# First attention of a two-block kernel: carried sums on VectorE, fewer triangle and mask matmuls

## The reference

```python
def stick_breaking_core(q, k, v):
    for start in range(0, seq, QBLK):            # QBLK = 128
        end = start + QBLK
        z = einsum('bhtd,bhsd->bhts', qf[:, :, start:end], kf[:, :, :end]) * scale
        earlier = arange(end)[None, :] < arange(start, end)[:, None]
        log_keep = where(earlier, log_sigmoid(-z), 0.0)
        csum = cumsum(log_keep, axis=-1)
        log_w = log_sigmoid(z) + (csum[..., -1:] - csum)
        w = where(earlier, exp(log_w), 0.0)
        outs.append(einsum('bhts,bhsd->bhtd', w, vf[:, :, :end]))
```

## Time and profile before

| | us |
|---|---|
| median of 3 runs | 1557.08 |
| lowest and highest | 1555.89, 1557.33 |
| span of the profiled execution | 1554.5 |
| PE busy in it | 1453.5 (94%) |
| ACT, POOL, DVE busy | 639.7, 760.4, 568.8 |

### The profile page before, as it was taken

One profiled execution on the slowest core, in us unless ns is written; L12 is line 12 of the kernel. 1 busy time (PEld: TensorE's weight loads), 2 busy tenths in 40 slices (PEclk: granted clock), 3 DMA queues, 4 the chain that ended last, 5 costly groups with the idle time before them and its releaser, 6 DMA issues.

```text
span 1554.5 us, 23458 instructions
## 1 busy us (share of the span) xinstructions
PE 1453.5 (94%) x8892; PEld 1181.3 (76%) x8892; DVE 568.8 (37%) x649; ACT 639.7 (41%) x1030; POOL 760.4 (49%) x591
## 2 busy tenths in 40 slices
PE   6999999898998999999999799599989999999995
PEld 6878778676776888888887477488867887888874
DVE  2024233244244333333122549732339334121222
ACT  4455465335335444444222645234334332222332
POOL 5734324245235655565555345753309554444563
PEclk9999999999999999999999899799999999999998
DMA  6412111022111332323333122100002332333322
GB/s 233 144 58 68 53 51 58 27 96 66 56 54 59 108 102 96 94 94 95 108 108 95 54 82 82 41 3 3 3 28 82 96 122 81 95 96 97 101 87 81
DMA packets 33772, 122.80 MB, mean 79 GB/s; under 512 B 3745, under 2 KB 4001, under 8 KB 33441
## 3 DMA queue, kind: packets, MB, share of 16 engines
q1 hardware_dynamic: 32832, 119.03, 23.7%
q10 hardware_dynamic: 864, 2.68, 0.5%
HBM read 119.59 MB, written 2.10 MB: 78 GB/s over the span
## 4 chain that ended last, share of the span: by engine, by line
PE 83%; DVE 9%; issue 4%; ACT 2%; POOL 2%; DMA 1%; DVEq 0%; ACTq 0%; POOLq 0%; SPq 0%
PE ps L421 19%; PE ps L423 19%; PE ps L422 19%; PE ps L529 3%; PE ps L943 2%; PE ps L447 2%; PE ps L448 1%; PE ps L1021 1%; PE ps L1022 1%; PE ps L1023 1%; PE ps L931 1%; PE ps L437 1%; PE ps L769 1%; PE ps L511 1%; PE ps L501 1%
## 5 line engine op out<-in xcount | busy, mean ns | idle before, releaser
L1501 POOL TENSOR_TENSOR w_lo<-stage,w_hi 128x512 fp32r<-128x512 f32 x434 | 604.1, 1415 | 664.7 <-ACT w_hi L1055 664.7
L1055 ACT ACTIVATE w_hi<-stage 128x512 fp32r<-128x512 f32 x434 | 249.8, 623 | 456.7 <-DMA stage<-w 452.2
L421 PE MATMUL ps<-x_hi,w_lo 128*128 128x512 f32 x1080 | 425.7, 394 | 6.0 <-POOL w_lo L1501 3.3
L423 PE MATMUL ps<-x_hi,w_hi 128*128 128x512 f32 x1080 | 421.2, 390 | 0.0
L422 PE MATMUL ps<-x_lo,w_hi 128*128 128x512 f32 x1080 | 420.9, 390 | 0.0
L421 PEld LDWEIGHTS ps<-x_hi,w_lo 128*128 128x128 f32 x1080 | 203.2, 188 | 52.7 <-issue 6.3
L422 PEld LDWEIGHTS ps<-x_lo,w_hi 128*128 128x128 f32 x1080 | 203.2, 188 | 43.3 <-issue 1.7
L423 PEld LDWEIGHTS ps<-x_hi,w_hi 128*128 128x128 f32 x1080 | 203.1, 188 | 42.7
L1807 DVE SCALAR_TENSOR_TENSOR conv<-ps,vcol,conv 128x511 f32<-128x511 f32 x44 | 33.0, 749 | 146.9 <-ACT conv L1205 146.9
L2043 DVE TENSOR_TENSOR bt<-gates,ps 128x512 f32<-128x512 f32 x24 | 16.4, 681 | 146.4 <-PE ps L1023 146.4
L421 PE MATMUL ps<-f_hi,w_lo 128*128 128x512 f32 x176 | 68.9, 391 | 0.0
(11 more groups left out here) (316 smaller groups left out, 2363.7 us busy)
## 6 DMA issues: line engine op xcount, KB each, us to landing
stage<-w SPq DMA_DIRECT2D x217, 512.0 KB, 3.5
H<-xT SPq DMA_DIRECT2D x1, 2048.0 KB, 13.7
outT<-H SPq DMA_DIRECT2D x8, 256.0 KB, 2.0
mem<-memT SPq DMA_DIRECT2D x2, 512.0 KB, 6.7
pool_n<-pool_count ACTq DMA_DIRECT2D x1, 1024.0 KB, 4.9
w_small<-small ACTq DMA_DIRECT2D x1, 512.0 KB, 5.0
con<-const ACTq DMA_DIRECT2D x1, 448.0 KB, 4.9
scan_keep<-const ACTq DMA_DIRECT2D x1, 256.0 KB, 9.2
```

Of the source, the lines that this page charges most:

```text
L421: pe.matmul(out, wl, hi(k), start=first, stop=False)
L423: mm = pe.matmul(out, wh, hi(k), start=False, stop=end)
L1055: act.activation(w_hi[:, b % RING, cols], stage[:, b % RING, cols], ACT.Copy).then_inc(whi_made, 1)
L1501: pool.tensor_tensor(w_lo[:, b % RING, cols], stage[:, b % RING, cols], w_hi[:, b % RING, cols].bitcast(F32), ALU.subtract).then_inc(wlo_m ...
```

## The change

The four regions stand in another order: region 3 (128 columns) now lies between region 0 and region 1 in the same bank as before. The parts of the change are:

- Masks: `never` is now two masks side by side, so that the first columns of regions 3 and 1, which are neighbours, are masked by one matmul of 256 columns: three matmuls a head in place of four. ACT makes the second copy of the mask once (a fifth step of `mask_made`).
- Sums within a block: the triangle `suffix` is applied to all 1280 columns in matmuls of 512, 512 and 256 columns, for the high and the low part (six). Region 3 into region 2 is added by two of 128 columns.
- Sums of later blocks: DVE adds keep of region 3 into the matching columns of region 2, and that into region 1, in place; then it splits these 640 columns into `later_hi` and `later_lo` (four new DVE instructions a head, each behind a semaphore of its own), and PE applies `every` to them, two matmuls of 256 and two of 384 columns, behind the new wait on `sb_llo`. A head has 12 matmuls in place of 20.
- `keep` has one buffer for both heads, since the buffer of head 1 is used by `later_hi` and `later_lo`. Head 1 may start only when `sb_llo` of head 0 is there, and the value copy stands behind `sb_llo` of head 1.
- The two DMAs of `levels` and `scan_keep` (used in the second block) move from the start of ACT's stream to behind the last pair.

The diff, without the lines that only declare semaphores:

```diff
@@ -69,8 +69,10 @@
 POOL_WINDOWS = (2, 4, 8, 16)
 
 
-REGION = {0: (0, 512), 1: (512, 384), 3: (896, 128), 2: (1024, 256)}
+REGION = {0: (0, 512), 3: (512, 128), 1: (640, 384), 2: (1024, 256)}
 SCORES = 1280
+DIAGONALS = [(0, P), (REGION[3][0], 2 * P), (REGION[2][0], P)]
+LATER0, LATER = REGION[1][0], 5 * P
 
 
 def build_block(nc, w, xT, memT, vec, const, small, pool_count, outT):
...
@@ -96,8 +98,8 @@
         vcol = at("vcol", [P, VEC], 99.5)
         suffix = at("suffix", [P, P], 24, F32R)
         every = at("every", [P, P], 24.5, F32R)
-        never = at("never", [P, P], 25, F32R)
-        ident_r = at("ident_r", [P, P], 25.5, F32R)
+        never = at("never", [P, 2, P], 25, F32R)
+        ident_r = at("ident_r", [P, P], 31, F32R)
         tmp = at("tmp", [P, 2, SEQ], 101.5)
         acc = at("acc", [P, SEQ], 105.5)
         acc2 = at("acc2", [P, SEQ], 107.5)
...
@@ -118,7 +120,9 @@
         vT_sb = at("vT_sb", [P, SEQ], A0 + 52)
         v_sb = at("v_sb", [P, NS, P], A0 + 54)
         soft = [at(f"soft{h}", [P, SCORES], 80 + 5 * h) for h in range(2)]
-        keep = [at("keep0", [P, SCORES], 90), at("keep1", [P, SCORES], A0 + 56)]
+        keep = at("keep", [P, SCORES], 90)
+        later_hi = [at("later_hi0", [P, LATER], 26, F32R), at("later_hi1", [P, LATER], A0 + 56, F32R)]
+        later_lo = [at("later_lo0", [P, LATER], 28.5, F32R), at("later_lo1", [P, LATER], A0 + 58.5, F32R)]
         keep_hi = [at(f"keep_hi{h}", [P, SCORES], A0 + 61 + 5 * h, F32R) for h in range(2)]
         keep_lo = [at(f"keep_lo{h}", [P, SCORES], A0 + 71 + 5 * h, F32R) for h in range(2)]
         xq = at("xq", [P, KB, SEQ], A0 + 48)
...
@@ -487,7 +495,7 @@
 
 
             E = EV0["sb"] + CREDIT
-            pe.wait_ge(mask_made, 4)
+            pe.wait_ge(mask_made, 5)
             pe.wait_ge(mv_taken, 8 + CREDIT)
             pe.wait_ge(h_split, 1)
 
...
@@ -512,23 +520,28 @@
                                   q_sb[64 * h:64 * h + 64, SEQ - n:SEQ], start=(i != 3), stop=False,
                                   skip_group_check=True)
                 for h in range(2):
-                    for i in range(NS):
-                        o, n = REGION[i]
-                        mm = pe.matmul(scores(h)[:, o:o + P], ident_r[:], never[:], start=False, stop=False,
-                                       skip_group_check=True)
+                    for o, n in DIAGONALS:
+                        mm = pe.matmul(scores(h)[:, o:o + n], ident_r[:], never[:].rearrange("p a n -> p (a n)")[:, 0:n],
+                                       start=False, stop=False, skip_group_check=True)
                     mm.then_inc(sb_scored, 1)
 
             def later_sums(g, h):
                 pe.wait_ge(sb_klo, 2 * g + (h + 1))
-                for i in range(NS):
+                for o, n in ((0, 512), (512, 512), (1024, 256)):
+                    for part in (keep_hi, keep_lo):
+                        pe.matmul(scores(h)[:, o:o + n], suffix[:], part[h][:, o:o + n], start=False, stop=False,
+                                  skip_group_check=True)
+                o, n = REGION[2]
+                for part in (keep_hi, keep_lo):
+                    pe.matmul(scores(h)[:, o + P:o + n], every[:], part[h][:, REGION[3][0]:REGION[3][0] + P],
+                              start=False, stop=(part is keep_lo), skip_group_check=True)
+                pe.wait_ge(sb_llo, 2 * g + (h + 1))
+                for i in (1, 0):
                     o, n = REGION[i]
-                    for s in range(i, NS):
-                        so, sn = REGION[s]
-                        m = suffix if s == i else every
-                        for part in (keep_hi, keep_lo):
-                            mm = pe.matmul(scores(h)[:, o + n - sn:o + n], m[:], part[h][:, so:so + sn],
-                                           start=False, stop=(s == NS - 1 and part is keep_lo),
-                                           skip_group_check=True)
+                    ro, rn = REGION[i + 1]
+                    for part in (later_hi, later_lo):
+                        mm = pe.matmul(scores(h)[:, o + P:o + n], every[:], part[h][:, ro - LATER0:ro - LATER0 + rn],
+                                       start=False, stop=(part is later_lo), skip_group_check=True)
                 mm.then_inc(sb_summed, 1)
 
             def turn_v(g):
...
@@ -1041,8 +1054,6 @@
         def _(act):
             act.dma_start(con[:], const[:, 0:C0["levels"]]).then_inc(params_in, 16)
             act.dma_start(vcol[:], vec).then_inc(params_in, 16)
-            act.dma_start(levels[:], const[:, C0["levels"]:C0["scan"]].rearrange("p (l n) -> p l n", n=HB)).then_inc(levels_in_s, 16)
-            act.dma_start(scan_keep[:], const[:, C0["scan"]:CONST]).then_inc(levels_in_s, 16)
             act.preload_act_table_set("natural_log_exp_and_others")
             act.sem_inc(evac, CREDIT)
 
...
@@ -1076,7 +1087,8 @@
             act.activation(suffix[:], C("suffix"), ACT.Copy).then_inc(mask_made, 1)
             act.activation(every[:], C("all"), ACT.Copy).then_inc(mask_made, 1)
             act.activation(ident_r[:], ident, ACT.Copy).then_inc(mask_made, 1)
-            act.activation(never[:], C("never"), ACT.Copy).then_inc(mask_made, 1)
+            act.activation(never[:, 0, :], C("never"), ACT.Copy).then_inc(mask_made, 1)
+            act.activation(never[:, 1, :], C("never"), ACT.Copy).then_inc(mask_made, 1)
 
             def pair(g, i, b, first=False, last=False):
 
...
@@ -1119,6 +1131,9 @@
                 pair(2 * i + 2, i, U0["sb"] + 8)
             pair(PAIRS - 1, 0, U0["sb"] + 3 * PAIRS - 1, last=True)
 
+            act.dma_start(levels[:], const[:, C0["levels"]:C0["scan"]].rearrange("p (l n) -> p l n", n=HB)).then_inc(levels_in_s, 16)
+            act.dma_start(scan_keep[:], const[:, C0["scan"]:CONST]).then_inc(levels_in_s, 16)
+
             def square_of(n, k, p):
 
                 act.wait_ge(y_made, k + (1 + CREDIT + BEFORE["y_made"][n]))
...
@@ -1689,13 +1704,25 @@
                 for h in range(2):
 
                     dve.wait_ge(sb_ln, 2 * g + (h + 1))
-                    dve.scalar_tensor_tensor(out=keep[h][:], in0=scores(h)[:, 0:SCORES], scalar=0.0, in1=soft[h][:],
+                    dve.scalar_tensor_tensor(out=keep[:], in0=scores(h)[:, 0:SCORES], scalar=0.0, in1=soft[h][:],
                                              op0=ALU.max, op1=ALU.add).then_inc(sb_keep, 1)
                     dve.wait_ge(sb_keep, 2 * g + (h + 1))
-                    dve.tensor_copy(keep_hi[h][:], keep[h][:]).then_inc(sb_khi, 1)
+                    dve.tensor_copy(keep_hi[h][:], keep[:]).then_inc(sb_khi, 1)
                     dve.wait_ge(sb_khi, 2 * g + (h + 1))
-                    dve.tensor_tensor(keep_lo[h][:], keep[h][:], keep_hi[h][:].bitcast(F32),
-                                      ALU.subtract).then_inc(sb_klo, 1)
+                    dve.tensor_tensor(keep_lo[h][:], keep[:], keep_hi[h][:].bitcast(F32), ALU.subtract).then_inc(sb_klo, 1)
+                    dve.wait_ge(sb_klo, 2 * g + (h + 1))
+                    o3, o2, o1 = REGION[3][0], REGION[2][0], REGION[1][0]
+                    dve.tensor_tensor(keep[:, o2 + P:o2 + 2 * P], keep[:, o2 + P:o2 + 2 * P], keep[:, o3:o3 + P],
+                                      ALU.add).then_inc(sb_from2, 1)
+                    dve.wait_ge(sb_from2, 2 * g + (h + 1))
+                    dve.tensor_tensor(keep[:, o1 + P:o1 + 3 * P], keep[:, o1 + P:o1 + 3 * P], keep[:, o2:o2 + 2 * P],
+                                      ALU.add).then_inc(sb_from1, 1)
+                    dve.wait_ge(sb_from1, 2 * g + (h + 1))
+                    dve.tensor_copy(later_hi[h][:], keep[:, LATER0:SCORES]).then_inc(sb_lhi, 1)
+                    dve.wait_ge(sb_lhi, 2 * g + (h + 1))
+                    dve.tensor_tensor(later_lo[h][:], keep[:, LATER0:SCORES], later_hi[h][:].bitcast(F32),
+                                      ALU.subtract).then_inc(sb_llo, 1)
+                    dve.wait_ge(sb_llo, 2 * g + (h + 1))
                 dve.wait_ge(sb_vturn, g + 1)
                 dve.tensor_copy(v_sb[:], ps[:, 0, :].rearrange("p (t n) -> p t n", t=NS)).then_inc(sb_v, 1)
                 dve.wait_ge(sb_ohi, g + 1)
```

More of the change, by code:

```diff
@@ L263, in build_block @@
         sb_klo = sem("sb_klo")
+        sb_from2 = sem("sb_from2")
+        sb_from1 = sem("sb_from1")
+        sb_lhi = sem("sb_lhi")
+        sb_llo = sem("sb_llo")
         sb_summed = sem("sb_summed")
```

## The result

| | before | changed |
|---|---|---|
| median of 4 runs, us | 1557.20 | 1574.73 |
| lowest to highest | 1555.89 to 1557.94 | 1573.33 to 1577.69 |
| span of the profiled execution | 1554.5 | 1571.6 |
| PE, DVE, ACT, POOL busy | 1453.5, 568.8, 639.7, 760.4 | 1451.1, 615.0, 639.9, 753.3 |

The ratio is 1.0116, 95% interval 1.0101 to 1.0131: slower by 17.5 us. The forecast was 1578, its range 1569 to 1588. The rows of PE sum to 2.4 us less, though they are longer where its clock is low, and the program is 17 us longer.

What follows compares the result with a forecast made beforehand. PE was taken to bound nearly every link. Seven pairs x (2.3 late DVE + 1.0 clock) = 23.1, -1.7, +0.2, -0.4 give +21.2, a span of 1575.7; the median 2.6 above makes 1578 us, range 1569 to 1588.

Steps and rivals of the forecast that it cites:

- strict alternation of DVE and POOL: Loop pairs: DVE casts, low parts and additions between SBUF tiles take turns with POOL's halves; late values make pairs 2.3 us longer.
- mutual slowing: Loop pairs: DVE and POOL only slowed while together, by 2.47/1.49; a pair would cost 1.7 us, not 2.3.
- second wait of 0.8 us: PE at head 1 of each loop pair: after eight matmuls it waits 0.8 us more, for later_lo.
- the clock's term: Loop pairs: PE's clock drops to 0.50 after idling 3.1 us; 1.0 us a pair taken, bounds 0 and 1.7.
- the rival in which the clock falls twice: Loop pairs: PE's clock falls twice or on the whole product, 7 x (2.3 + 1.7 to 2.5), 1583 to 1589; chance 0.12.
- the holding by POOL: Loop pairs: POOL's weight halves block DVE instructions ahead of the value copy, priced at 1.9 us a pair.
- without any holding: Lower bound for loop pairs: DVE never blocked by POOL, values done at 185.35, a pair 0.4 us shorter; total 1552.
- The last pair: Sums inside the output product: values are ready before PE needs them, so PE keeps its gain of 1.7 us.
- The start: Ahead of the attention: fifth mask copy +0.2 us before the first scores, two DMAs moved from ACT's queue -0.4 us.
- the clock holds: Rival, loop pairs: eight matmuls between the waits keep PE's clock up; 7 x 2.3 = 16.1, less 1.9: 1571; chance 0.14.
- PE keeps its gain: Rival, loop pairs: values ready before PE asks, DVE's chain 4.1 us shorter than counted; -13.8 us, 1543; chance of faster 0.05.
- Holding is milder: Rival, loop pairs: POOL's blocking of DVE costs 1.7 us or less a pair, no clock fall; 1561 to 1567; chance 0.09.

Runs made afterwards that it cites:

- the kernel with the carried sums late: Changed kernel with two keep buffers, DVE's four new instructions a head behind the value copy, PE's last four matmuls a head inside the third product, loop pairs only: 1544.61 us.
- the kernel with twelve idle matmuls: Changed kernel plus twelve useless 512-column matmuls on PE between turning the values and the sums of head 1, in the seven loop pairs: 1570.52 us, ratio 1.0078.

## Why the prediction was right

Each step of it has its measured number, in the fourth pair, from its first keep. Low part of head 1 done: 12.70 predicted, 12.59 measured. later_lo of head 1: 14.88 and 14.75. Value copy: 15.60 and 15.57. Wait of PE for keep_lo: 3.1 and 2.86. DVE's busy time: 14 or more and 15.6. The strict alternation of DVE and POOL gave the cast of 640 and later_lo of head 0 the ends 6.20 and 8.05; measured 6.16 and 7.99. So the exclusive lock (the Trainium skill, SBUF — State Buffer, Who interferes with whom), and not a mutual slowing, is what the timeline shows: under the latter, as the prediction worked it out, the chain would have ended 0.7 us sooner, and a pair cost 1.7; it costs 2.46 without the clock. The cast of 640 is plainer still: it took 1.47 us for 0.49, where a slowing by 2.47/1.49 would make it 0.81.

Two of the signs that it named came out otherwise. The second wait of 0.8 us was to show in seven pairs and shows in one, with 0.42, since PE comes late by its low clock. And the low clock was to fall on the product behind; in the fourth pair it falls on the sums and is over when the product starts. Where the chain's end is the same, the length of the pair is too (30.53 with the clock at 1.00; the prediction's 28.08 + 2.3 is 30.38).

That the clock's term agrees, 1.0 a pair for 0.94, is in part luck. No pair costs that: five cost 0.3 to 0.6, and two cost 1.9 and 2.5, as the rival in which the clock falls twice had it (1.7 to 2.5). With another share of such pairs the same mechanism gives another time. One figure among the rivals doesn't follow from the prediction's own count: it calls the holding by POOL 1.9 us a pair, while its two chains end at 188.04 and 185.35, 2.7 apart; measured, 2.5. And without any holding a pair was to be 0.4 shorter than before; it was 0.1 shorter (27.97).

The sum, term by term, in spans. Seven pairs: +23.1 predicted, +23.8 measured, of which the chain 17.2 (16.1 predicted) and the clock 6.6 (7.0). The last pair, from its first keep to the first sum of the output product: -1.7 predicted; it took 313.98 - 284.76 = 29.22 before and 333.70 - 305.87 = 27.83, -1.4. The start, first keep at 85.57 for 88.25: -2.7 measured where the prediction had +0.2 and -0.4. Behind the output product: nothing predicted, -2.6 measured. These make 17.1, the 1571.6 - 1554.5 of the spans, for 21.2 predicted. The start and the part behind the output product were put 2.5 and 2.6 too high, the pairs and the last pair together 1.0 too low. (The median of the runs lies 3.1 above the span now, not 2.6, which gives 0.5 of it back.)

The start was mis-sized because the clock there differs between the two executions, which no step had considered. Before and after, the same stretch:

```profile
65.00:68.30 3.30, 0.94 (x5) 0.61 (x5) 0.85 (x2) 2.22 (x7) 3.08 (x3) 1.00 0.52 159
68.30:71.70 3.40, 3.40 (x10) 2.62 (x9) 0.00 (x0) 1.15 (x2) 2.71 (x3) 0.50 0.00 0
```

```profile
65.00:68.30 3.30, 1.85 (x8) 1.43 (x9) 0.42 (x1) 2.86 (x9) 2.97 (x3) 1.00 0.41 139
68.30:71.70 3.40, 3.40 (x16) 2.81 (x16) 0.00 (x0) 0.00 (x0) 2.07 (x2) 1.00 0.00 0
```

Before, ten matmuls fit in the second stretch, after sixteen: six matmuls of 0.23, 1.4 us. In the stretch ahead PE had been busy for 0.94 us before the change and for 1.85 after it. In the profiles of the other kernels with moved DMAs the first keep stands anywhere from 86.5 to 89.3, so the -1.3 that remains for the DMAs and the mask copy is within that scatter. What the DMAs do is seen at PE's first matmul: it starts 0.08 to 0.36 us earlier than 11.44 in the eight profiles with the DMAs moved, where the prediction took 0.4; the run of the DMA edit alone gives -0.3 to -3.1 for the whole time.

Behind the output product it is the same. The profile before has one more stretch of half clock in the second block, absent after:

```profile
1010.30:1013.80 3.50, 3.50 (x54) 3.38 (x51) 0.00 (x0) 1.41 (x5) 3.48 (x7) 0.51 0.02 5
```

From DVE's row at 1004.68 (`diag`) to that at 1015.83 (`XT`), about this stretch, 11.15 us pass before and 9.30 after. The change is not the cause: the kernel before with only its DMAs moved has 9.31 there, and the kernel with the carried sums late, whose code there is the changed kernel's, has 11.14. So 1.85 of the 2.6 is which of two courses an execution took; the other 0.8 is a sum of small differences of both signs, and its cause stays open.

Of the rivals, "the clock holds" (1571) is what the kernel with twelve idle matmuls came to, 1570.5. "PE keeps its gain" asked for the values 4.1 us sooner; moving the new work behind the value copy did that, and gave 1544.6 where 1543 had been worked out. "Holding is milder" fell with the rows of POOL.

## What to carry to other kernels

Work moved to an engine that is 64% idle is free only where its stream has a gap: here the idle time lay ahead of and behind the chain that PE waits for, whose lead was 1.65 us, and the 4.3 us of new work stood inside it. The same instructions behind the last one that PE needs soon cost PE nothing and kept most of its gain, 1.54 of 1.7 us a pair; ask first what stands behind a new instruction on its engine, then what runs beside it and can hold it. When a wait of nearly 3 us appears on PE, count its clock too: here 0.3 to 2.5 us a pair on top of 2.46 for the late chain, 0.94 in the mean. And before a difference of 1 to 3 us between two profiles is put down to a change, look where their clocks were low: the first keep stands anywhere from 85.57 to 89.26 us here in the profiles of seven kernels that are the same, or nearly so, up to it.

## What the runs showed of the hardware

Two-input VectorE instructions and casts on SBUF tiles ran strictly in turn with GpSimd's splits: counted that way, the ends of the pair's chain come out within 0.13 us (12.70, 14.88 and 15.60 counted, 12.59, 14.75 and 15.57 measured). A VectorE instruction that reads PSUM and one SBUF tile was not held (1.49 beside POOL). What a turn costs doesn't shrink with the instruction: the cast of 640 columns took 1.47 for 0.49, later_lo 1.80 for 0.82, the addition of 256 took 1.40 for 0.42, while the larger cast of 1280, which met the last half of POOL's work under way, took 1.42 for 0.83. And useless matmuls in a wait made the kernel faster (1570.5 for 1574.7): with them the granted clock was 1.00, the upper level of 2.4 GHz, in all seven pairs, and without them 0.89 to 0.95.
